# The mLSTM steps of a diffusion trunk's odd layer, run in slots between the projections, with one small buffer padded

## The reference

```python
def step(carry, inp):
    Cm, nv, m = carry
    qc, kc, vc, li, lf = inp
    b = jnp.cumsum(lf, axis=1)
    b_end = b[:, -1]
    w_end = b_end[:, None] - b + li
    m_new = jnp.maximum(b_end + m, jnp.max(w_end, axis=1))
    decay = jnp.exp(b_end + m - m_new)
    wk = jnp.exp(w_end - m_new[:, None])[..., None] * kc
    C_new = decay[..., None, None] * Cm + jnp.einsum("blhv,blhk->bhvk", vc, wk)
    n_new = decay[..., None] * nv + jnp.sum(wk, axis=1)
    dmat = jnp.where(causal, b[:, :, None] - b[:, None] + li[:, None], -jnp.inf)
    inter = b + m[:, None]
    m_q = jnp.maximum(jnp.max(dmat, axis=2), inter)
    s = jnp.einsum("bqhd,bkhd->bqkh", qc, kc) * jnp.exp(dmat - m_q[:, :, None])
    w_inter = jnp.exp(inter - m_q)
    num = einsum(s, vc) + w_inter[..., None] * einsum(Cm, qc)
    den = jnp.sum(s, axis=2) + w_inter * einsum(nv, qc)
    h = num / jnp.maximum(jnp.abs(den), jnp.exp(-m_q))[..., None]
```

## Time and profile before

| | us |
|---|---|
| median of 3 runs | 1949.94 |
| lowest and highest | 1946.14, 1950.98 |
| profiled execution, its own time | 1950.95 |
| its span | 1949.2 |

### The profile page before, as it was taken

How to read it: one execution, slowest core, us unless ns; L and a number is a source line. 1 busy time by engine, 2 the same in 40 slices (tenths; PEclk the granted TensorE clock), 3 DMA queues, 4 the chain that set the end, 5 groups by cost and what they waited for, 6 DMA issues and landing times.

```text
span 1949.2 us, 25181 instructions
## 1 busy us (share of the span) xinstructions
PE 1844.9 (95%) x10094; PEld 1491.5 (77%) x10094; DVE 887.5 (46%) x1375; ACT 614.6 (32%) x824; POOL 36.3 (2%) x72
## 2 busy tenths in 40 slices
PE   3999999999889999999999999999998998899996
PEld 1788778868544668888888688888877988589996
DVE  2433323345878552333334533333344455865555
ACT  2322122233445332212222322222223133244342
POOL 0000000000001000000000000000000000000000
PEclk7999999999899989999999999999998999999998
DMA  8522452243148353222213422232232224045553
GB/s 337 218 86 87 173 194 86 75 164 124 44 163 306 137 193 131 82 96 103 106 64 111 169 90 92 81 108 108 68 126 111 87 88 151 1 176 186 179 178 103
DMA packets 39108, 252.39 MB, mean 129 GB/s; under 512 B 4465, under 2 KB 5873, under 8 KB 14449
## 3 DMA queue, kind: packets, MB, share of 16 engines
q1 hardware_dynamic: 29232, 179.91, 26.3%
q0 software_dynamic: 9792, 71.31, 9.5%
HBM read 250.15 MB, written 1.05 MB: 129 GB/s over the span
## 4 chain that ended last, share of the span: by engine, by line
PE 87%; DVE 7%; ACT 2%; DMA 2%; issue 2%; SPq 0%; ACTq 0%; DVEq 0%
PE ps L396 26%; PE ps L398 26%; PE ps L397 26%; PE ps L432 3%; PE ps L596 1%; DMA xT<-in_xT 1%; DVE w_lo L1083 1%; DVE y L1266 1%; PE ps L570 1%; PE ps L743 1%; ACT w_hi L805 1%; PE ps L456 1%; PE ps L579 1%; DVE t_ring L1144 1%; PE ps L710 0%
## 5 line engine op out<-in xcount | busy, mean ns | idle before, releaser
L396 PE MATMUL ps<-hn_hi,w_hi 128*128 128x512 f32 (+2 forms) x1784 | 646.3, 362 | 12.4 <-DVE hn_lo L1160 8.2
L397 PE MATMUL ps<-hn_lo,w_hi 128*128 128x512 f32 (+2 forms) x1784 | 640.4, 359 | 0.0
L398 PE MATMUL ps<-hn_hi,w_lo 128*128 128x512 f32 (+2 forms) x1784 | 640.1, 359 | 0.0
L1083 DVE TENSOR_TENSOR w_lo<-raw,w_hi 128x2048 fp32r<-128x2048 f32 (+2 forms) x184 | 377.0, 2049 | 569.7 <-ACT w_hi L805 569.6
L805 ACT ACTIVATE w_hi<-raw 128x2048 fp32r<-128x2048 f32 (+2 forms) x184 | 316.6, 1721 | 823.5 <-PE ps L398 814.2
L396 PEld LDWEIGHTS ps<-hn_hi,w_hi 128*128 128x128 f32 (+1 forms) x1784 | 338.8, 190 | 77.3 <-issue 24.4
L398 PEld LDWEIGHTS ps<-hn_hi,w_lo 128*128 128x128 f32 (+1 forms) x1784 | 338.9, 190 | 50.5 <-issue 0.3
L397 PEld LDWEIGHTS ps<-hn_lo,w_hi 128*128 128x128 f32 (+1 forms) x1784 | 339.1, 190 | 48.4 <-issue 0.7
L396 PE MATMUL ps<-a_hi,w_hi 128*128 128x512 f32 (+1 forms) x704 | 258.9, 368 | 1.8 <-DVE a_lo L1198 1.8
L398 PE MATMUL ps<-a_hi,w_lo 128*128 128x512 f32 (+1 forms) x704 | 258.5, 367 | 0.0
L397 PE MATMUL ps<-a_lo,w_hi 128*128 128x512 f32 (+1 forms) x704 | 258.5, 367 | 0.0
(11 more groups left out here) (181 smaller groups left out, 1182.6 us busy)
## 6 DMA issues: line engine op xcount, KB each, us to landing
raw<-in_w_up SPq DMA_DIRECT2D x88, 1024.0 KB, 4.9
mod_raw<-in_mod_w POOLq DMA_DIRECT2D x68, 1024.0 KB, 7.1
raw<-in_w_downA SPq DMA_DIRECT2D x32, 768.0 KB, 4.3
raw<-in_w_downB SPq DMA_DIRECT2D x32, 640.0 KB, 3.9
raw<-in_w_od_in SPq DMA_DIRECT2D x16, 1024.0 KB, 4.8
raw<-in_w_ev_in SPq DMA_DIRECT2D x7, 1024.0 KB, 4.9
mod_raw<-in_mod_w SPq DMA_DIRECT2D x4, 1024.0 KB, 11.0
raw<-in_w_ev_out SPq DMA_DIRECT2D x4, 1024.0 KB, 4.9
```

The lines of the kernel that those rows point to most:

```text
L396: pe.matmul(o, lh, rh, start=first, stop=False)
L397: pe.matmul(o, lh, rl, start=False, stop=False)
L398: return pe.matmul(o, ll, rh, start=False, stop=last)
L1083: dve.tensor_tensor(w_lo[:, u0 % 2, 0:n], raw[:, u0 % 2, 0:n], w_hi[:, u0 % 2, 0:n], ALU.subtract).then_inc(lo_made, 1)
```

## The change

Five things change, all but the last in the odd mixer.

1. The weights are put in another order: units 0..7 are key and value of head 0, of head 1 and so on.
2. The mLSTM steps no longer stand behind unit 15. A table `SLOTS` puts each key turn, state, score and output in a slot inside or behind a unit n = 4..14 (four slots in a unit of 96 matmuls, two in a unit of 48). Steps use the PSUM bank pairs 6/7 and 4/5 in turn; a step waits until the step two before it has left its pair. Outputs are made head by head.
3. The weighted keys are made by ACT, up to two steps ahead, in a ring of their own (in `sd`); `scaled_out` writes to `t_ring`. The root and the scaling of the heads come within unit 15, before its gate.
4. The gate maxima come from scans: the 32 columns of `a` are turned into rows, DVE runs two max scans over them, three small PE operations bring the results back. 8 of the 12 spreads and the `maxima` function go. The 16 bias additions become 3.
5. `sel` is allocated with 32 columns, of which 8 are used.

```diff
-        sel = sb("sel", [P, 8])
+        sel = sb("sel", [P, 32])[:, 0:8]
+        wk_ring = sd[:].rearrange("p (a b) -> p a b", a=2)
-        OUTS = [(2, d, h) for d in range(2) for h in range(HM)] + [(3, d, h) for d in range(2) for h in range(HM)]
-        STATES = [(s, d, h) for s in range(3) for d in range(2) for h in range(HM)]
+        OUTS = [(s, d, h) for h in range(HM) for s in (2, 3) for d in range(2)]
+        STATES = [(s, d, h) for h in range(HM) for s in range(2) for d in range(2)]
+        STATES += [(2, d, h) for h in range(HM) for d in range(2)]
+        SLOTS = {
+            4: steps("a0|a1|a2|a3"),
+            5: steps("a4|a5|a6|a7"),
+            6: steps("k0|k1|a8|a9"),
+            7: steps("a10|a11|k2|"),
+            8: steps("a12 a13 k3|a14 a15"),
+            9: steps("s0|o0 o1"),
+            10: steps("a16 a17|o2 o3 s1"),
+            11: steps("o4 o5|a18 a19 s2"),
+            12: steps("o6 o7 o8|o9 a20"),
+            13: steps("a21 s3 o10|o11 o12 o13"),
+            14: steps("a22 a23|o14 o15"),
+        }
+        ORDER = [step for n in sorted(SLOTS) for slot in SLOTS[n] for step in slot]
+        PAIR = {step: 6 - 2 * (i % 2) for i, step in enumerate(ORDER)}
...
+            def pair_free(step):
+                i = ORDER.index(step)
+                if i == 1:
+                    pe.wait_ge(hid_made, 4)
+                if i >= 2:
+                    kind, n = ORDER[i - 2]
+                    if kind == "state":
+                        pe.wait_ge(st_made, n + 1)
...
+            def state_up(n, to):
+                s, d, h = STATES[n]
+                pe.wait_ge(wk_made, n + 1)
+                pe.wait_ge(unit_evac, U["od_in"] + 2 * h + 2)
...
+            def outputs(n, to):
+                pe.wait_ge(sT_made, h + 1)
+                pe.wait_ge(st_made, 4 * h + 2 + d + 1 if s == 2 else 16 + 2 * h + d + 1)
...
+            for n in range(1, 8):
+                u = U["od_in"] + n
+                begin(u)
+                for i in range(4):
+                    for k in range(KT):
+                        last = three(...)
...
+                    if (n, i) == (1, 2):
+                        pe.wait_ge(a_cols, 1)
+                        pe.transpose(ps[0:32, 6, 0:P], GATE["a"].rearrange("p d s h -> p (d s h)"), ident)\
+                            .then_inc(rows_mm, 1)
+                    if (n, i) == (2, 0):
+                        pe.wait_ge(scan_made, 1)
...
+                    slot(n, i)
+            for n in range(8, 16):
+                u = U["od_in"] + n
+                begin(u)
+                for k in range(KT):
...
+                    if k == 3:
+                        slot(n, 0)
+                last.then_inc(unit_mm, 1)
+                slot(n, 1)
```

ACT and DVE go through the units in the same order: in iteration n they round unit n+2, read unit n, and then serve the steps of the slots of unit n+1. On ACT:

```diff
+            def weighted(n):
+                s, d, h = STATES[n]
+                if n >= 2:
+                    act.wait_ge(st_up, n - 1)
+                act.wait_ge(unit_evac, U["od_in"] + 2 * h + 1)
+                act.activation(wk_ring[:, n % 2, :], k_tok[:, STEP_TILE[d][s], h, :], ACT.Copy,
+                               scale=GATE["val"][:, d, s, h:h + 1]).then_inc(wk_made, 1)
...
+            for n in range(16):
                 head_of(U["od_in"] + 2 + n)
...
+                for step in steps_of(n + 1):
+                    kind, m = step
+                    for a in AHEAD.get(step, ()):
+                        weighted(a)
+                    if kind == "keys":
+                        keys_turned(m, PAIR[step])
+                    elif kind == "out":
+                        scaled_out(m, PAIR[step])
+                if n == 14:
+                    sum_squares(14)
+                    sum_squares(15).then_inc(ss_made, 1)
+                    act.wait_ge(ss_made, 1)
+                    act.activation(ms_cols[:, 1, :], ms_cols[:, 0, :], ACT.Sqrt, bias=eps[:], scale=1.0 / DH)\
+                        .then_inc(hsd_made, 1)
```

On DVE:

```diff
+            def running():
+                rows, first, last_on, top = (sq[0:32, 0, P * e:P * (e + 1)] for e in range(4))
+                link(dve.tensor_copy(rows, ps[0:32, 6, 0:P]))
+                link(dve.tensor_tensor_scan(first, rows, rows, -3e38, ALU.max, ALU.max))
+                dve.tensor_tensor_scan(last_on[:, ::-1], rows[:, ::-1], rows[:, ::-1], -3e38, ALU.max, ALU.max)
+                dve.tensor_scalar(top[:, 0:32], ident[0:32, 0:32], first[:, P - 1:P], None, ALU.mult)\
+                    .then_inc(scan_made, 1)
...
+                if n == 14:
+                    dve.wait_ge(hsd_made, 1)
+                    link(dve.reciprocal(ms_cols[:, 1, :], ms_cols[:, 1, :]))
+                    for h in range(HM):
+                        for i in (h, HM + h):
+                            dve.tensor_scalar(xT[:, i, LAT:TOK], xT[:, i, LAT:TOK], ms_cols[:, 1, i:i + 1], None,
+                                              ALU.mult).then_inc(hnorm, 1)
+                for step in steps_of(n + 1):
+                    kind, m = step
+                    if kind == "state":
+                        new_state(m, PAIR[step])
+                    elif kind == "scores":
+                        scored(m, PAIR[step])
+                    elif kind == "out":
+                        head_output(m, PAIR[step])
```

More of the change, by code:

```diff
@@ L686, in _ @@
             last.then_inc(gates_mm, 1)
[L688 to L720, removed]
+            def pair_free(step):
[6 more added lines that the diff above has]
+                        pe.wait_ge(st_made, n + 1)
+                    elif kind == "keys":
+                        pe.wait_ge(kT_made, n + 1)
+                    elif kind == "scores":
+                        pe.wait_ge(sT_made, n + 1)
+                    else:
+                        pe.wait_ge(out_made, n + 1)
@@ new lines, in state_up, with turn_keys @@
+            def state_up(n, to):
+                s, d, h = STATES[n]
+                pe.wait_ge(wk_made, n + 1)
+                pe.wait_ge(unit_evac, U["od_in"] + 2 * h + 2)
+                for kt in range(2):
+                    last = pe.matmul(ps[:, to + kt, 0:DH + 1], wk_ring[:, n % 2, kt * P:(kt + 1) * P],
+                                     v_tok[:, STEP_TILE[d][s], h, :], start=True, stop=True)
+                last.then_inc(st_up, 1)
+            def turn_keys(h, to):
+                pe.wait_ge(unit_evac, U["od_in"] + 2 * h + 1)
@@ L730, in _ @@
                     for kt in range(2):
-                        last = pe.matmul(ps[:, 4 + i, h * P:(h + 1) * P], kT[:, 2 * h + kt, i * P:(i + 1) * P],
+                        last = pe.matmul(ps[:, to, i * P:(i + 1) * P], kT[:, 2 * h + kt, i * P:(i + 1) * P],
                                          qT[:, 2 * h + kt, i * P:(i + 1) * P], start=(kt == 0), stop=(kt == 1))
                 last.then_inc(st_mm, 1)
[L735 to L745, removed]
@@ L766, in _, with slot @@
-            for n in range(8):
-                state_up(16 + n)
-            for n in range(8):
-                outputs(8 + n)
+            def slot(n, i):
+                for step in SLOTS[n][i] if n in SLOTS else ():
+                    kind, m = step
+                    pair_free(step)
+                    if kind == "state":
+                        state_up(m, PAIR[step])
+                    elif kind == "keys":
+                        turn_keys(m, PAIR[step])
+                    elif kind == "scores":
+                        scores_of(m, PAIR[step])
+                    else:
+                        outputs(m, PAIR[step])
@@ new lines, in _ @@
+            for n in range(8, 16):
+                u = U["od_in"] + n
+                begin(u)
+                for k in range(KT):
+                    for b in range(2):
+                        last = three(ps[:, bank(u, b), 0:LAT], weights(u, k * DH + b * P, k * DH + b * P + P),
+                                     (hn_hi[:, k, 0:LAT], hn_lo[:, k, 0:LAT]), k == 0, k == KT - 1)
+                    if k == 3:
+                        slot(n, 0)
+                last.then_inc(unit_mm, 1)
+                slot(n, 1)
@@ L1539, in new_state, with head_output @@
                 last.then_inc(st_made, 1)
-            def head_output(n):
+            def head_output(n, at):
                 s, d, h = OUTS[n]
@@ L1691, in layout @@
     w = od_w_in[0]
-    put["w_od_in"] = np.concatenate([tiles(w[:, D * i:D * (i + 1)], DH) for i in (1, 2, 0, 3)], axis=0)
+    queries, keys, values, gate = [tiles(w[:, D * i:D * (i + 1)], DH) for i in range(4)]
+    put["w_od_in"] = np.concatenate([np.stack([keys, values], axis=1).reshape(2 * HM, P, -1), queries, gate], axis=0)
     put["w_od_gate"] = tiles(w[:, 4 * D:], 4 * HM)[0]
```

314 lines of the change are left out of this document (153 added, 161 removed).

## The result

| | before | after |
|---|---|---|
| median, us | 1950.46 (4 runs) | 1923.53 (4 runs) |
| lowest and highest | 1946.14, 1951.27 | 1918.44, 1927.58 |
| profiled execution, its own time | 1950.95 | 1918.44 |
| its span | 1949.2 | 1916.7 |

The ratio of the times is 0.9862, 95% interval [0.9842, 0.9881]: 1.4% faster and clear of the noise, with 1923.53 against 1923.5 predicted. The profiled execution of after is the lowest of its four, so I compare stretches of the traces and not its total. Later the same kernel ran again beside the experiments: 1922.23 us, ratio 0.9855 [0.984, 0.987]. Two executions of experiments ran far slower, at mean granted clocks of 0.655 and 0.645 (2636.05 us with the padding alone, 3156.68 us with all steps behind); they are left out of the ratios, though not of those two medians.

A forecast was written before the change was run, and what follows sets the result against it. PE is full during projections; behind the last one, steps alternate between PE and DVE. Steps and gates sum to -16.4 us and padding to -11.1, so 1950.95 becomes 1923.5; the forecast's own range is 1914 to 1932.

The forecast's parts named there:

- The stage: Odd mixer behind the last projection: 71.0 us without projections go, 47.9 us of PE work come back between projections.
- Spreads, turns, scans: Gate maxima in the odd mixer: 8 of 12 spreads go, -6.9 us; small turns +0.6; scans 0, bound +3.
- New stalls: PE waits for DVE at slots in units 8, 9 and 13: 2.6, 1.2 and 1.2 us, sum +5.0.
- Handover: Passing from step to step on PE, 44 steps at 0.05 us each: +2.2, bound 0 to +12.
- The gap to od_out: Last projection to `od_out`: PE gap 7.0 us, plus 1.5 for slower matmuls behind it; sum +8.5, bounds 4.4 and 13.
- The padding: `a_hi` and `a_lo` start at a multiple of 64 bytes: -12.2 us at 512 columns, +1.1 at 256, sum -11.1.
- The rest up to the odd mixer: Stretch ahead of the odd mixer's first row: 12.2 us less by padding and 0.6 by gate additions.
- Half clock in the slots: Rival: gaps of some 5 us in eleven units with slots halve the clock, 23 us more, total 1956; chance 0.05.

The follow-up runs named there:

- all steps behind: The changed kernel with all its steps moved to one place behind the last projection, root and scaling behind them; 1932.65 us, ratio 0.9907 to before.
- reading first: The changed kernel with DVE, in units 7 to 11 of the odd mixer, reading unit n before splitting the weights of unit n+2; 1917.34 us, ratio 0.9828.
- tail edit: Against the kernel that reads first: ACT rounds unit 17's weights behind the first three heads, DVE splits them behind all heads; 1916.09 us, ratio 0.9829.
- moved latent columns: The changed kernel with hn and a in columns 16 to 272 instead of 0 to 256 where only latents are worked on; 1918.93 us, ratio 0.9841.

## Why the prediction was right

*The stage is worth 71.0 and gives back 47.9.* Right in both halves: the stage is gone, states cost 0.87 (0.88), outputs 0.43 + 0.87 (1.31). The run with all steps behind shows the same 0.43 + 0.87 for outputs there, and that the move gains only PE's idle time, which is what the sum rests on.

*Spreads, turns, scans.* 7.8 us measured alone, 8.4 by the sum. The scans, bounded at 0 to +3, cost nothing.

*New stalls.* 2.81, 1.06 and 0.9 (the last at L771, behind a state) against 2.6, 1.2 and 1.2. They came from the cause named, weight splitting ahead of reading: reading first takes the first two away.

*Handover.* +2.2 is the term that failed, though within its bounds: states stand exactly one quarter unit and 0.87 apart.

*The gap to od_out.* 7.2 us against 7.0, with a wait of 3.96 against "nearly 4". The half clock behind it shows in `od_out`, whose 192 matmuls took 24.0 us from first to last start instead of 23.0: 1.0 of the 1.5 I had added.

Put together, without that 1.5: 213.0 - 71.0 + 47.9 - 6.9 + 0.6 + 5.0 - 2.1 + 2.2 + 7.0 = 195.7. Less the handover it is 193.5, and 193.8 was measured.

*The padding.* The mechanism was right and its rule half right. -12.2 at 512 columns is what the streams show (1584 x 0.0076 = 12.0). "A multiple of 64 bytes" was wrong: 64 beyond a multiple of 128 gives 0.2333. That the change gains all of it is luck: its 96 bytes happen to reach a multiple of 128, where `hn` and the weights also start. By the prediction's own rule 32 bytes would have done, and they give 1584 x 0.001 = 1.6 us at 512 columns instead of 12. With the rule on cachelines of 16 bytes in the Trainium skill, SBUF — State Buffer, Specifications, by which nothing would be gained, these runs do not agree: each start tried lies at a multiple of 16, and the spacings differ by 3%.

*The rest up to the odd mixer.* 15.7 against 12.8 is one execution. In the second profile of after the odd mixer starts 5.8 us later (1485.11), so this stretch gained 9.9 there; the median of the runs is between the two.

*Half clock in the slots* had 0.05 for 23 us. It does occur, behind the longest stall in the slots, in one profile of after in two, and costs 3.4 us there, of which eight state matmuls show 1.8. I had looked at one row where a wait of 2.1 us left the clock full and took waits up to 2.6 as harmless.

*The total.* 1923.53 against 1923.5 is closer than the parts are. The first profile of after has a span 32.5 us below that of before (1949.2 to 1916.7), where 27.5 were forecast, the second 22.3 (1926.9). The mechanism is borne out by the stretches; that the median hits the forecast to 0.1 us is luck.

## What to carry to other kernels

Where the busy engine is full on both sides of a move, the move is worth only the idle time that it removes: here 65 us less in a stage were 9 to 10 us. Before code is reordered, compare the spacing of equal instructions in different stages; a difference of 3% between two streams of one shape was worth 11 us for one line of padding, and two unused gaps of 32 bytes lost 24. After any edit of a buffer list, look at the starts of all streamed and stationary operands again, and at the distance between them: here 0 modulo 256 was best at 512 columns. And on an engine that serves another, read results first and prepare inputs second, as long as the inputs still come in time: 3.4 us of stalls for a reordering.

The kernel that reads first is the fastest here, 1917.34 us (1916.09 with the tail edit as well, which is no different). Reading first together with moved latent columns and unmoved weights was not run.

## What the runs showed of the hardware

- Spacing of fp32r matmuls at full clock depends on where both operands start. 512 columns, weights at a multiple of 128 bytes: 0.2267 us for a start at 0 modulo 128, 0.2343 at 32, 0.2333 at 64 and at 96; with the weights at 64, 0.2333 for `hn` at 0. 256 columns: 0.1201 where both starts are equal, 0.1179 for `hn` at 64 and weights at 0. What the parts of the memory do there is not shown.
- Behind a wait of PE of one length (2.81 us) the granted clock was 1.00 in two profiles and 0.56 to 0.57 in two.
- Two executions of one program differ by 10 us. The table of cores of the first and the second profile of after:

```profile
core 0: 1916.7 us, clock 0.974
```

```profile
core 0: 1926.9 us, clock 0.969
```

If the clock is either full or half, that is 1916.7 x 0.026 x 2 = 100 us at half against 1926.9 x 0.031 x 2 = 119: an estimate of 20 us more, each costing up to half of itself. The odd mixer, up to `od_out`, shows 3.4 us of it (193.8 against 197.2); that the clock makes up the 5.8 us ahead of the odd mixer is argued and not shown. The mean clock alone doesn't tell the time either: two executions of before took 1951.46 us at 0.925 and 1951.52 at 0.970. So a term of a few us can't be read from totals of single executions, but it can from stretches of a trace at full clock.
